# A static order that also places loads, masks, key copies and the second half of the linear attention's norms

## The reference

```
xn = rms_norm(h, pre_norm)
proj = xn @ w_in                       # q, k, v, gates of two mixers
o_gla = gla_mixer(q, k, v, log_a)      # linear attention with decay, 4 heads of 128
o_gla = rms_norm(o_gla, gla_out_norm) * silu(g_z)
o_nsa = nsa_mixer(...)                 # 8 heads: compressed, selected and window branch
o_nsa = o_nsa * silu(n_z)
h = h + rms_norm(concat(o_gla, o_nsa) @ w_out, post_norm)
h = h + rms_norm((p @ ple_proj) * sigmoid(h @ ple_gate), ple_norm)
```

## Time and profile before

| | |
|---|---|
| median of 3 runs | 840.2 us (839.7 to 841.76) |
| the profiled execution, whole | 841.0 us |
| its span in the profile | 839.2 us |
| TensorE busy | 811.7 us (97%) |
| VectorE busy | 527.0 us (63%) |
| ScalarE busy | 449.4 us (54%) |
| GpSimd busy | 386.1 us (46%) |
| granted TensorE clock, mean | 0.997 of full speed |

### The profile page before, as it was taken

The page is one execution under the profiler, slowest core; times in us unless marked ns, Lnnn a source line. Parts: engine busy times, 40 slices in busy tenths (PEclk is TensorE's granted clock), DMA queues, the critical chain, the costliest instruction groups (busy, mean ns, idle before and its releaser), DMA issues.

```text
span 839.2 us, 12231 instructions
## 1 busy us (share of the span) xinstructions
PE 811.7 (97%) x4514; PEld 677.6 (81%) x4514; DVE 527.0 (63%) x922; ACT 449.4 (54%) x925; POOL 386.1 (46%) x354
## 2 busy tenths in 40 slices
PE   7999999999999999999999999999999999999995
PEld 7878898888988788878678888778778888887884
DVE  2771449871761804487999999999971243444436
ACT  4602144212333014758999999999982343526434
POOL 3302118335141121556476766666635455553554
PEclk9999999999999999999999999999999999999998
DMA  9511011101111011252200000000039323232237
GB/s 312 103 51 50 26 36 50 51 26 51 27 41 48 20 44 38 76 140 72 51 1 2 2 1 2 1 2 1 1 116 331 117 95 101 82 97 70 98 109 242
DMA packets 39917, 58.35 MB, mean 70 GB/s; under 512 B 11281, under 2 KB 17713, under 8 KB 39858
## 3 DMA queue, kind: packets, MB, share of 16 engines
q1 hardware_dynamic: 39570, 56.52, 22.2%
q0 software_dynamic: 288, 1.05, 0.8%
HBM read 49.16 MB, written 5.25 MB: 65 GB/s over the span
## 4 chain that ended last, share of the span: by engine, by line
PE 72%; DVE 13%; ACT 8%; issue 3%; POOL 3%; DMA 0%; DVEq 0%; SPq 0%; ACTq 0%; POOLq 0%
PE psum L1007 48%; DVE pT_lo L2282 4%; DVE p_slc L2254 3%; PE psum L1122 3%; ACT pT_hi L1654 2%; PE psum L1299 2%; PE psum L1033 2%; ACT p_win L1636 2%; ACT p_slc L1636 1%; PE psum L928 1%; PE psum L927 1%; PE psum L929 1%; ACT p_slc L1667 1%; PE psum L1277 1%; PE psum L1172 1%
## 5 line engine op out<-in xcount | busy, mean ns | idle before, releaser
L1781 POOL TENSOR_TENSOR w_lo<-w_raw,w_hi 128x512 fp32r<-128x512 f32 x126 | 179.8, 1430 | 331.9 <-ACT w_hi L1430 331.5
L1430 ACT ACTIVATE w_hi<-w_raw 128x512 fp32r<-128x512 f32 x126 | 79.4, 634 | 312.1 <-PE psum L1007 300.1
L1007 PE MATMUL psum<-w_hi,xT_hi 128*128 128x512 f32 x256 | 101.0, 395 | 1.7 <-DVE gla_state_b L2159 1.7
L1007 PE MATMUL psum<-w_hi,xT_lo 128*128 128x512 f32 x256 | 99.7, 389 | 0.0
L2282 DVE TENSOR_TENSOR pT_lo<-psum,pT_hi 128x512 fp32r<-128x512 f32 (+1 forms) x148 | 95.2, 655 | 7.2 <-ACT pT_hi L1654 5.1
L1007 PE MATMUL psum<-w_lo,xT_hi 128*128 128x512 f32 x256 | 99.6, 389 | 0.0
L1654 ACT ACTIVATE pT_hi<-psum 128x512 fp32r<-128x512 f32 (+1 forms) x148 | 82.5, 568 | 6.7 <-PE psum L1299 5.8
L1277 PE MATMUL psum<-kT,qT_hi_lo 128*128 128x384 f32 (+3 forms) x192 | 67.4, 353 | 0.4 <-DVE neg_max L2254 0.3
L1837 POOL TENSOR_SCALAR p_slc<-p_slc,gate_over_sum 128x512 f32<-128x512 f32 (+7 forms) x40 | 64.3, 1617 | 1.5
L1278 PE MATMUL psum<-kT,qT_hi_lo 128*128 128x384 f32 (+3 forms) x192 | 60.6, 328 | 0.0
L1636 ACT ACTIVATE p_slc<-p_slc,neg_max 128x512 f32<-128x512 f32 (+7 forms) x80 | 58.1, 728 | 2.8 <-DVE neg_max L2254 2.3
(11 more groups left out here) (295 smaller groups left out, 1963.3 us busy)
## 6 DMA issues: line engine op xcount, KB each, us to landing
w_raw<-in_w_in SPq DMA_DIRECT2D x56, 256.0 KB, 2.7
w_raw<-in_w_out SPq DMA_DIRECT2D x32, 256.0 KB, 2.7
w_raw<-in_ple_gate SPq DMA_DIRECT2D x32, 256.0 KB, 2.6
x_tok<-in_x SPq DMA_DIRECT2D x8, 512.0 KB, 6.5
h_tok<-in_x SPq DMA_DIRECT2D x8, 512.0 KB, 5.8
kT<-kT SPq DMA_DIRECT2D x12, 256.0 KB, 3.8
out<-h_tok SPq DMA_DIRECT2D x6, 512.0 KB, 5.6
w_raw<-in_ple_proj SPq DMA_DIRECT2D x8, 256.0 KB, 2.6
```

The lines of the kernel that those rows point to most:

```text
L1007: mm = pe.matmul(out, lhs, rhs, start=(first and n == 0), stop=(final and n == 2))
L1430: act.activation(w_hi(i)[:, 0:w], w_in(i)[:, 0:w], ACT.Copy).then_inc(s_whi, 1)
L1781: pool.tensor_tensor(w_lo(i)[:, 0:w], w_in(i)[:, 0:w], w_hi(i)[:, 0:w].bitcast(F32), ALU.subtract).then_inc(s_wlo, 1)
```

## The change

The second `inverse_rms` of the linear attention (tiles 4 to 7) leaves its place between the weight splits of `nzA` 5 and 6, and the four multiplications by it leave VectorE: both become GpSimd operations of the list, `gla_rms` and `gla_gate`. The loads of `nzB` 3 to 7, the load of the masks, and the key copies become SyncE operations of the list, and SyncE walks it too. The masks are waited for where they are first used, no longer at the head of the first two steps. The small tile `gla_ss` moves to another place in SBUF, and TensorE waits for all eight `gla_z` tiles before the transposes ahead of `woA`. Two start times of the list change (VectorE 3000 to 2600 ns, ScalarE 3000 to 4200 ns), and the list of the whole attention is drawn anew.

```diff
--- before.py
+++ after.py
@@ -195,6 +195,7 @@
     RG = sm("gate_over_sum", [P, 4 * 48])
     CMX = sm("cmp_max", [P, 2, GRP])
     ident = CT[:, C_ID:C_ID + P]
+    GSS = sb("gla_ss", [P, 3, NT * GH], F32, small[0])
     W2 = sm("cmp_w2", [P, 2, DH])
     PB = sm("cmp_pos", [P, 2, 16])
     CB = sm("cmp_pos_bias", [P, 2])
@@ -215,7 +216,6 @@
     ATT = sb("gla_att", [P, NT, GH, P], F32, R6 + 16384)
     GM = sb("gla_masks", [P, len(LEVELS), P], F32, R4 + 8192)
     DG = sb("gla_diag", [P, NT, GH], F32, R4 + 20480)
-    GSS = sb("gla_ss", [P, 3, NT * GH], F32, R4 + 22048)
     GBL = sb("gla_decay_last", [P, 2, NT], F32, R4 + 22432)
     KTN = sb("gla_k_dec_tok", [P, NT, 256], F32, R7 + 8192)
     GSA = sb("gla_state_a", [P, 4, 2, 2 * P], F32, R4 + 12288)
@@ -598,12 +598,17 @@
         for k in range(KD):
             if k >= 2:
                 ops["gate_hi", k] = "A", 630, 5
-                after["gate_hi", k] = [("gate_mm", k - 3)]
+                after["gate_hi", k] = [("gate_mm", k - 3), ("load", k)]
                 ops["gate_lo", k] = "G", 1310, 0
                 after["gate_lo", k] = [("gate_hi", k)]
             if k < WHOLE:
                 ops["gate_mm", k] = "P", 2880, 5
                 after["gate_mm", k] = [("gate_lo", k)]
+            if k >= RAW:
+                ops["load", k] = f"load {k}", 3000, 0
+                after["load", k] = [("gate_lo", k - RAW)]
+        ops["masks", 0] = "masks", 4500, 0
+        after["masks", 0] = [("stack_turn", stacks.index(("q", 3, 0)))]
         for b in range(4):
             ops["gate_end", b] = "P", 680 * (KD - WHOLE) + 160, 5
             after["gate_end", b] = [("gate_lo", KD - 1)]
@@ -630,8 +635,11 @@
             after["stack_lo", u] = [("stack_hi", u)]
             if kind == "k":
                 pair = stacks[u][1]
-                ops["key_copy", 2 * half + pair] = f"D{2 * half + pair}", 3200, 0
-                after["key_copy", 2 * half + pair] = [("stack_lo", u)]
+                n = 2 * half + pair
+                ops["even_keys", n] = f"even keys {n}", 3800, late
+                after["even_keys", n] = [("stack_lo", u)]
+                ops["odd_keys", n] = f"odd keys {n}", 2800, late
+                after["odd_keys", n] = [("even_keys", n)]
         for s, step in enumerate(steps):
             nk = span(*step[1:])[1]
             freed = pair_freed(s, 0)
@@ -640,7 +648,7 @@
             if step[2] == 0:
                 ops["cscore", s] = "P", 600, s
                 after["cscore", s] = after_pair(freed) + [("stack_lo", stacks_needed(step) - 1)]
-                for kind, eng, dur, *deps in (("csum", "V", 680, ("cscore", s), reuse), ("cmask", "G", 670, ("csum", s)),
+                for kind, eng, dur, *deps in (("csum", "V", 680, ("cscore", s), reuse), ("cmask", "G", 670, ("csum", s), ("masks", 0)),
                                               ("cmax", "V", 400, ("cmask", s)), ("csub", "G", 610, ("cmax", s)),
                                               ("cexp", "A", 410, ("csub", s)), ("gate", "V", 620, ("cexp", s)),
                                               ("gates", "G", 200, ("gate", s)), ("cscale", "G", 610, ("gates", s))):
@@ -651,9 +659,9 @@
                 n = GRP * s + g
                 ops["score", n] = "P", 0.86 * nk + 290, s
                 after["score", n] = after_pair(pair_freed(s, g)) + [("stack_lo", stacks_needed(step) - 1)] \
-                    + [("key_copy", 2 * half + pair) for pair, half in keys_needed(step)]
+                    + [("odd_keys" if step[0] else "even_keys", 2 * half + pair) for pair, half in keys_needed(step)]
                 ops["mask_max", n] = "V", 1.04 * nk + 158, s
-                after["mask_max", n] = [("score", n), reuse]
+                after["mask_max", n] = [("score", n), reuse, ("masks", 0)]
                 ops["exponent", n] = "A", 0.845 * nk + 375, s
                 after["exponent", n] = [("mask_max", n)]
                 e = scaler[step[2]][g]
@@ -684,10 +692,16 @@
             if not last:
                 ops["gated", j] = "G", 680, 3 * j + 2
                 after["gated", j] = [("output", j)]
-        kinds = ["values", "half", "output", "gated", "low", "high", "turn", "gate", "gates", "cmax", "cexp", "csub", "cmask", "cscale", "scaleV", "scaleA", "scaleP",
+        ops["gla_rms", 0] = "G", 3400, 2
+        after["gla_rms", 0] = []
+        for t in range(4, NT):
+            ops["gla_gate", t] = "G", 1350, 40
+            after["gla_gate", t] = [("gla_rms", 0)]
+        kinds = ["gla_rms", "gla_gate", "values", "half", "output", "gated", "low", "high", "turn", "gate", "gates", "cmax", "cexp", "csub", "cmask", "cscale", "scaleV", "scaleA", "scaleP",
                  "exponent", "csum", "mask_max", "cscore", "score", "gate_z", "gate_mul", "first_mul", "gate_sig", "stack_lo", "stack_hi", "stack_turn",
-                 "gate_lo", "gate_hi", "gate_mm", "gate_end", "key_copy"]
-        overlap = {"P": 162, "V": 83, "A": 103, "G": 28, "D0": 0, "D1": 0, "D2": 0, "D3": 0}
+                 "gate_lo", "gate_hi", "gate_mm", "gate_end",
+                 "load", "masks", "even_keys", "odd_keys"]
+        overlap = {"P": 162, "V": 83, "A": 103, "G": 28}
         hand = {"PV": 37, "PA": 36, "VP": 55, "AP": 55, "GP": 80, "AV": 32, "VA": 35, "VG": 80, "AG": 80, "GV": 60, "GA": 60}
         after = {op: [d for d in after[op] if d in ops] for op in ops}
         users = {op: [] for op in ops}
@@ -710,7 +724,7 @@
 
             needs, frees = (users, after) if backwards else (after, users)
             queue = {k: sorted((n for kind, n in ops if kind == k), reverse=not backwards) for k in kinds}
-            free = {} if backwards else {"V": 3000, "A": 3000}
+            free = {} if backwards else {"V": 2600, "A": 4200}
             missing, ready = {op: len(needs[op]) for op in ops}, dict.fromkeys(ops, 0)
             end, line = {}, []
             heads = {kind: (kind, queue[kind].pop()) for kind in kinds if queue[kind]}
@@ -720,7 +734,7 @@
                     if missing[op]:
                         continue
                     eng = ops[op][0]
-                    at = max(free.get(eng, 0) - overlap[eng], ready[op])
+                    at = max(free.get(eng, 0) - overlap.get(eng, 0), ready[op])
                     key = at + weight * rank[op], at
                     if best is None or key < best[0]:
                         best = key, kind
@@ -836,7 +850,7 @@
             sp.dma_start(PB[:, n], a[pe][0].rearrange("(l a) d -> (a d) l", a=2),
                          allow_slow_non_contiguous=True).then_inc(s_small, 16)
         sp.dma_start(GGN[:], a["gla_out_norm"][0].partition_broadcast(P)).then_inc(s_small, 16)
-        for i in range(KD + RAW, piece0[cidx["woA"]]):
+        for i in range(KD + RAW, piece0[cidx["nzB"]] + RAW):
             load_piece(i)
             if i == piece0[cidx["gqk"]] + 6:
                 sp.wait_ge(s_rt, 2)
@@ -849,17 +863,16 @@
                 sp.wait_ge(s_la, 4)
                 sp.wait_ge(s_gtr, 1)
                 sp.dma_start(GM[:], a["gla_masks"].rearrange("p (l j) -> p l j", j=P)).then_inc(s_gm, 16)
-            if i == piece0[cidx["nzB"]] + 4:
-                even_keys(0, 0)
-                even_keys(1, 0)
-        sp.wait_ge(s_qtr, 6)
-        sp.dma_start(MK[:], a["masks"]).then_inc(s_mk, 16)
-        odd_keys(0, 0)
-        odd_keys(1, 0)
-        for pair in range(2):
-            even_keys(pair, 1)
-        for pair in range(2):
-            odd_keys(pair, 1)
+        for kind, n in timeline:
+            if kind == "load":
+                load_piece(piece0[cidx["nzB"]] + n)
+            elif kind == "masks":
+                sp.wait_ge(s_qtr, stacks.index(("q", 3, 0)) + 1)
+                sp.dma_start(MK[:], a["masks"]).then_inc(s_mk, 16)
+            elif kind == "even_keys":
+                even_keys(n % 2, n // 2)
+            elif kind == "odd_keys":
+                odd_keys(n % 2, n // 2)
 
 
         sp.wait_ge(s_pv, len(units))
@@ -1341,6 +1354,8 @@
 
         pe.wait_ge(s_ttr, masked_count(len(steps) - 1, GRP - 1))
         for u in range(8):
+            if u == 0:
+                pe.wait_ge(s_gend, NT)
             if u == 6:
                 pe.wait_ge(s_oev, 2 * NT)
             for i in range(4):
@@ -1788,6 +1803,20 @@
             pool.tensor_tensor(halves(x, z, True), halves(x, z, True), halves(GQK[:, 2:4], z, True),
                                ALU.mult).then_inc(s_dec_x, 1)
 
+        def gla_rms(half):
+
+            ts = slice(4 * GH * half, 4 * GH * half + 4 * GH)
+            pool.wait_ge(s_og, 4 * half + 4)
+            inverse_rms(GSS[:, 1, ts], GSS[:, 2, ts], GSS[:, 0, ts], GDV, 4 * GH, s_orms)
+
+        def gate_gla(t):
+
+            z = GZ[:, t].rearrange("p (h d) -> p h d", h=GH)
+            r = GSS[:, 2, t * GH:t * GH + GH].unsqueeze(2).to_broadcast([P, GH, GDV])
+            pool.wait_ge(s_orms, 2)
+            pool.wait_ge(s_gprod, t + 1)
```

(22 more changed lines are left out.)

## The result

The changed kernel takes 843.8 us (median of 5 runs, 843.0 to 844.6), the kernel before 840.2 (839.7 to 841.8): the ratio is 1.0041, 95% interval 1.003 to 1.0052. That is 3.6 us slower, where 838.8 was said and 842.3 was the upper end. The profiled execution took 843.83 us, its span is 842.0, against 839.2 before; so the trace has 2.8 us to account for.

What follows compares the result with a forecast made beforehand. TensorE was taken to pace the kernel to 397 us, then three engines 95% busy at once. 841.0 - 1.26 = 839.7, median 0.8 below: 838.9, less 0.1 for earlier masks: 838.8 us, range 835.3 to 842.3.

Steps and rivals of the forecast that it cites:

- The norm leaves its place: GpSimd, before the split of `nzA` 6: TensorE's wait at 359.27 goes, 1.26 us gained.
- GpSimd's work: Norm and four multiplications at 1.3 to 1.8 us each; the split of `nzB` 2 on time, 370.8 to 372.3: no loss.
- VectorE's relief: Four multiplications, 5.74 us, leave VectorE under the matmuls of `nzA`; counted as 0 for TensorE.
- their place under the norm: The four `first_mul` right behind `gate_z`, mostly beside GpSimd's norm, which was said not to stretch VectorE's work.
- Masks: SyncE: masks issued at about 372, first `mask_max` at about 377 instead of 380.6; worth 0 up to 397.
- the last product of `nzB`: TensorE, end of the projections, near 397 us: said to come 1.3 us earlier.
- The loads of `nzB` 6 and 7, which wait for the splits of 3 and 4 anyway: SyncE, loads passed by the masks, splits at 375 and 377.5; high parts wait for TensorE, so 0.
- a late load: Condition for being wrong: a copy or load queued behind the masks is late; no size given.
- I take 0: New order over the whole attention: 0, between bounds of 4.0 us better and 4.5 us worse.
- the rival given 0.15: Slower: from 397 to 618 the new order makes TensorE wait for `low` more often, 0.9 us each; chance 0.15.
- Its bound of five more waits of 0.9, 4.5 us: Worst case for the new order: five more waits for `low` of the longest kind, 5 x 0.9 = 4.5 us.
- Nothing makes a redraw better on the chip: Argument for the slower case: list lengths are estimates and the same search found the last order; chance 0.15.

Runs made afterwards that it cites:

- e1: The changed kernel with the kernel before's written-out order and SyncE sequence; only the norm and its four multiplications stand on GpSimd as changed: 841.1 us, ratio 0.9999.
- e5: The list of e1 with VectorE's four `first_mul` moved ahead of the first key split, all else in place: 840.8 us, ratio 0.9996.
- e3: As e1, but with the changed kernel's SyncE sequence (masks and second key copy ahead of the loads of `nzB` 6 and 7): 840.7 us, ratio 0.9998.
- e7: As e6, but the new order only up to the last `gate_end`, the order of before for all that is left: 839.1 us, ratio 0.9974.
- e6: The changed kernel with the second key pair's copy moved behind the load of `nzB` 6, masks still ahead of both: 842.7 us, ratio 1.0029.
- after_seed3: The changed kernel with the seed of its list search set to 3, nothing else changed: 840.0 us, ratio 0.9988.

## Why the prediction was wrong, point by point

**The norm leaves its place: right.** -1.26 was said; the end of `nzA` comes 1.3 to 1.4 us earlier, in every kernel that has this part.

**GpSimd's work: right, in the new order.** The multiplications take 1.03 to 1.30 us, not 1.3 to 1.8; the split of `nzB` 2 is done at 369.3, about 1 us ahead of the earliest time said (the 0.6 of the span's start taken off). That VectorE's relief is worth 0 fits, though no run tests it alone. What was left out is that the move costs something when the `first_mul` stand beside it: e1 gives back 1.1 of its 1.4 us, e5 only 0.6. The prediction leaned on their place under the norm, and in the changed kernel they stand there, four in 2.48 us.

The page SBUF — State Buffer of the Trainium skill, section Who interferes with whom, has a GpSimd instruction that reads SBUF and one of VectorE's with two SBUF inputs exclude each other. e1 agrees for the multiplications and the weight splits: its four `first_mul` beside them took 1.22 to 1.78 us each. The changed kernel doesn't agree for the norm: three `first_mul` start inside the 2.90 us of GpSimd's power and take 0.68 us each, as one does alone.

**Masks: right.** They are issued at 371.1 and the first `mask_max` runs at 376.0, where 372.1 and 377 were said (0.6 of the span's start again). But the last product of `nzB`, said to come 1.3 us earlier, comes no earlier than before, counted from the first projection: the late load has taken the shift by then.

**"The loads of `nzB` 6 and 7, which wait for the splits of 3 and 4 anyway": the first step that failed.** The load is issued at 373.8, no later than the 375 said. But its landing was put at nothing ("whose high parts wait for TensorE"), and where the loads before took 2.7 us in the median it took 5.8, behind the masks and the copy. ScalarE's high part waited for the load and not for TensorE, and TensorE stood 1.45 us, more than the norm's shift. The prediction had named a late load among what would make it wrong, and had given it no price. The 5.1 us of the load behind the key copies in the trace of before could have given it one. e3 adds that the lateness costs more than 0.3 us only with the new order behind it.

**"I take 0" for the new order: the second step that failed, and the larger.** It costs 3.9 us behind the first value matmul. By the records TensorE is idle 11.4 - 8.8 = 2.6 us more behind 397; the rest of the 3.9 they don't resolve, since the ends of matmuls are modelled. This is the rival given 0.15, and in part its mechanism: TensorE waits more for `low` (+1.8 us, from 11 to 13 times), and besides for `mask_max` (+1.0) and once for a scaling on VectorE (0.8), which it didn't name, while a few other waits shrink. Its bound of five more waits of 0.9, 4.5 us, holds the 3.9, but by luck: only two waits for `low` were added. e7 shows that the order behind the last `gate_end` makes this loss, and nothing ahead of it.

**The sum again.** -1.4 (norm) - 0.3 (gained between there and the first values, as e6 shows) + 1.4 (late load) + 3.9 (order) = +3.6 at `woA`, as measured; by the spans, 2.8. The second step alone (e6, 842.7) already passes the upper end of 842.3; the late load alone (e3, 840.7) doesn't.

**"Nothing makes a redraw better on the chip": right for the draw that was measured, doubtful beyond it.** The kernel before had a good draw of a search whose two others gave 851 and 854; the changed search gives 839.0 to 843.8 in three draws, and the first of them is its worst. The masks are one thing that the changed search does better, by the waits of 6.2 and 7.8 us shown above. Three draws a side show a spread, not its mean.

**Open.** Why the new tail costs 3.4 us by itself and only 1.4 behind the new middle, and which moves in either make it, wasn't settled; that the loss consists of waits between saturated engines is argued from the timelines. That the two orders differ in many places at once is all that the cuts leave.

## What to carry to other kernels

When an order comes out of a random search, a change of the search's rules is also a new draw: compare several draws of each side, and splice the old and the new order to see which stretch wins; here the spliced one (839.1 us) and another draw (839.0) are both faster than the kernel before. What a transfer is queued behind belongs in its price, and so does whoever stands behind its reader in that engine's order: a load that was as late cost 1.4 us in one order and 0.3 at most in another. An earlier arrival is worth something only if each engine's order behind it can keep it.

## What the runs showed of the hardware

- A load of a weight piece took 2.7 us from issue to landing in the median before. Directly behind the masks it took 3.0 (e6, `nzB` 6). Behind a key copy inside SBUF it took 3.9 (e6, `nzB` 7), 5.1 (before, `nzB` 5), and with the masks in flight too 5.8 (after) and 6.5 (e3). At the same place in the queue it took only 4.1 in after_seed3, so the place alone doesn't set the time.
- On GpSimd a multiplication of 128x512 with one factor for each row and head (four a row) took 1.03 us, the weight split of the same size with two full operands 1.29; beside VectorE's `first_mul` they took up to 1.49 and 1.74. GpSimd's power on 128x16, 2.90 us, didn't lengthen VectorE's work beside it (0.68 each, after).
- Where the three engines are saturated and the order is that of before, a shift was carried through within 0.2 us: e7 is 1.40 us early at the first values and 1.40 at `woA`, 221.5 us later, e5 0.80 and 0.76, e3 0.03 and 0.03, e1 0.28 and 0.13.
